# The order of projection, feed-forward openings and second mixer in a kernel of three transformer blocks

## What is computed

```python
def conv_ffn(h, w_up, conv_w, conv_b, w_down):
    u = h @ w_up                                   # 1024 -> 2 * 2816
    u = lax.conv_general_dilated(u, conv_w ...) + conv_b   # 3 taps, per channel, causal
    gate, val = jnp.split(u, 2, axis=-1)
    return (jax.nn.silu(gate) * val) @ w_down      # 2816 -> 1024

for i in range(2):                                 # i = 0: "fox", i = 1: "mla"
    h = rmsnorm(x, norm_mix[i])
    p = h @ w_in
    o_mix = mixer(p[..., :-MEM_WIDTH])             # 12 heads
    o_mem = memory_cross(p[..., -MEM_WIDTH:], k_mem, v_mem, ...)   # 4 heads, 256 keys
    x = x + jnp.concatenate([o_mix, o_mem], axis=-1) @ w_out[i]
    x = x + conv_ffn(rmsnorm(x, norm_ffn[i]), ...)
# the third block
x = x + 0.5 * swiglu(rms_norm(x, g_ffn1), ...)
x = x + mix(rms_norm(x, g_mix)) @ w_out            # window attention, 31-tap convolution, memory attention
x = x + 0.5 * swiglu(rms_norm(x, g_ffn2), ...)
```

## Time and profile before

| | |
|---|---|
| median of 3 runs | 2228.88 us (2228.45 to 2229.82) |
| the profiled execution: its own time | 2224.88 us |
| its span in the profile | 2223.1 us |
| TensorE busy | 2117.9 us, 95% |
| VectorE busy | 1274.8 us, 57% |
| ScalarE busy | 952.9 us, 43% |
| GpSimd busy | 33.7 us, 2% |
| mean granted TensorE clock | 0.982 |
| DMA | 187.36 MB, 84 GB/s on average |

### The profile page before, as it was taken

How to read it: one execution, slowest core, us unless ns; L and a number is a source line. 1 busy time by engine, 2 the same in 40 slices (tenths; PEclk the granted TensorE clock), 3 DMA queues, 4 the chain that set the end, 5 groups by cost and what they waited for, 6 DMA issues and landing times.

```text
span 2223.1 us, 30649 instructions
## 1 busy us (share of the span) xinstructions
PE 2117.9 (95%) x11378; PEld 1759.9 (79%) x11378; DVE 1274.8 (57%) x2212; ACT 952.9 (43%) x1912; POOL 33.7 (2%) x71
## 2 busy tenths in 40 slices
PE   6999998999999798989999999999998889999999
PEld 6888786888889676768888888888888667888887
DVE  6645567746764775567367544434447865543442
ACT  6645544423445764444244343223344564332331
POOL 0000001000000010000000000000001000000000
PEclk9999999999999899989999999999999999999999
DMA  6212132332333010222333233333232112333332
GB/s 203 73 53 58 49 91 62 102 103 90 95 100 105 15 39 29 71 76 95 100 94 100 95 95 100 95 97 98 90 100 62 39 30 81 105 99 91 103 96 91
DMA packets 101670, 187.36 MB, mean 84 GB/s; under 512 B 11408, under 2 KB 12048, under 8 KB 101264
## 3 DMA queue, kind: packets, MB, share of 16 engines
q1 hardware_dynamic: 101520, 185.39, 27.5%
HBM read 183.25 MB, written 2.10 MB: 83 GB/s over the span
## 4 chain that ended last, share of the span: by engine, by line
PE 47%; DVE 3%; ACT 2%; issue 1%; POOL 0%; DVEq 0%; ACTq 0%; POOLq 0%
PE PSA L1541 15%; PE PSA L1542 14%; PE PSA L1543 14%; PE PSA L1559 1%; PE PSA L1560 1%; PE PSA L1561 1%; DVE RS L1694 1%; DVE WL L1705 0%; ACT PP L2043 0%; ACT WH L1974 0%; PE PSA L1648 0%; PE PSA L1663 0%; DVE CV L1694 0%; PE PSA L1630 0%; DVE XT L1846 0%
## 5 line engine op out<-in xcount | busy, mean ns | idle before, releaser
L1705 DVE TENSOR_TENSOR WL<-RAW,WH 128x512 fp32r<-128x512 f32 x681 | 459.2, 690 | 470.7 <-ACT WH L1974 447.1
L1974 ACT ACTIVATE WH<-RAW 128x512 fp32r<-128x512 f32 x681 | 414.7, 626 | 485.5 <-PE PSA L1543 407.1
L1541 PE MATMUL PSA<-HNh,WH 128*128 128x512 f32 x1440 | 566.3, 393 | 28.5 <-DVE CV L1694 21.2
L1542 PE MATMUL PSA<-HNl,WH 128*128 128x512 f32 x1440 | 562.9, 391 | 0.0
L1543 PE MATMUL PSA<-HNh,WL 128*128 128x512 f32 x1440 | 562.8, 391 | 0.0
L1541 PEld LDWEIGHTS PSA<-HNh,WH 128*128 128x128 f32 x1440 | 272.0, 189 | 89.6 <-DVE CV L1694 22.0
L1542 PEld LDWEIGHTS PSA<-HNl,WH 128*128 128x128 f32 x1440 | 272.0, 189 | 57.3 <-issue 1.2
L1543 PEld LDWEIGHTS PSA<-HNh,WL 128*128 128x128 f32 x1440 | 271.8, 189 | 56.9
L1541 PE MATMUL PSA<-Gh,WH 128*128 128x512 f32 x704 | 274.3, 390 | 0.9 <-DVE Gl L1869 0.9
L1542 PE MATMUL PSA<-Gl,WH 128*128 128x512 f32 x704 | 273.9, 389 | 0.0
L1543 PE MATMUL PSA<-Gh,WL 128*128 128x512 f32 x704 | 273.9, 389 | 0.0
(11 more groups left out here) (253 smaller groups left out, 2478.1 us busy)
## 6 DMA issues: line engine op xcount, KB each, us to landing
RAW<-in_w SPq DMA_DIRECT2D x681, 256.0 KB, 2.6
XT<-in_x SPq DMA_DIRECT2D x8, 256.0 KB, 5.3
MT<-in_mem SPq DMA_DIRECT2D x2, 1024.0 KB, 6.4
out_x<-XT SPq DMA_DIRECT2D x8, 256.0 KB, 2.1
PAR<-in_par SPq DMA_DIRECT2D x1, 207.0 KB, 7.2
CB<-in_cb SPq DMA_DIRECT2D x1, 100.0 KB, 7.1
PAR<-in_par SPq DMA_DIRECT2D x1, 84.5 KB, 2.0
CONST<-in_const SPq DMA_DIRECT2D x1, 65.0 KB, 5.3
```

Source lines behind the costliest of these rows:

```text
L1541: pe.matmul(out, wh, xh, start=(a["start"] and c == 0), stop=False)
L1542: pe.matmul(out, wh, xl, start=False, stop=False)
L1705: dve.tensor_tensor(l[:, :], r[:, :], h[:, :], ALU.subtract).then_inc(done.sem("split.dve"), 1)
L1974: act.activation(h[:, :], r[:, :], ACT.Copy).then_inc(done.sem("split.act"), 1)
```

## The change

- Projection: chunks are closed in the order 0, 4, 1, 5, 2, 6, 3, 7 rather than 0 to 7. A chunk's square is put 5 beats and its addition 6.2 beats behind the closing of the chunk, rather than all behind the last chunk. The additions are chained in the order in which they are written, and `total` waits for the last of them.
- ffn 0, 1 and 3: one pair of groups is opened before the first `scale` rather than two, and `total` comes behind two groups rather than four (ffn 2 had it so). In later pairs each group is followed by its own `scale` and convolution, rather than both groups first.
- Second mixer: the memory queries' group comes before the latent group, its helper banks are 4 to 7, and memory attention begins directly behind the latent group.
- The value half of a key/value widening is emptied by VectorE (`vevac`) rather than by ScalarE, behind the key half; 12 instructions.
- `pbcast` is issued behind the values and the turns of that moment (`sums`), and the step of the attention sink earlier.
- Third mixer: some turns come 2.5 to 5 beats later.

```diff
 def out_parts(first, late):
-    return ([(c, first, late) for c in range(OPEN)] + [(c, late, 8) for c in range(OPEN)]
-            + [(c, first, 8) for c in range(OPEN, 8)])
+    return [(c, first, late) for c in range(OPEN)] + [x for c in range(OPEN) for x in ((c, late, 8), (OPEN + c, first, 8))]
...
             def add(self, c):
-                step("feed", (self.name, c), norm=self, c=c, sq=("feed", self.name, c))
+                step("feed", (self.name, c), norm=self, c=c, sq=("feed", self.name, c), last=self.adds[-1:])
+                self.adds.append(c)
...
-                if i == 3:
-                    need([("precip.dve", jkey)])
-                    aux = aux_bank(("pbcast", jkey), [("pspread.act", ckey)])
-                    step("pbcast", jkey, S=PSTAT[pstats.of[jkey]], bank=aux)
...
                 step("pvals", key, job=job, i=i, jkey=jkey, t=t)
-                return 0.3 * job.tiles[i][1] / 128 + (0.8 if i == 3 else 0)
+                return 0.3 * job.tiles[i][1] / 128
+
+            def sums(self, n, i):
...
+                step("pbcast", jkey, S=PSTAT[pstats.of[jkey]], bank=aux)
...
                     cost += self.values(*turned) if turned else 0
                     cost += self.turn(*scored) if scored else 0
+                    cost += self.sums(*turned) if turned else 0
...
                 norm.part(c, norm.free, 1.3)
+                after(5, lambda: norm.square(c))
+                after(6.2, lambda: norm.add(c))
...
             until([("part.dve", (norm.name, KC - 1))], 0)
-            for c in range(KC):
-                after(0.5 + 1.3 * c, lambda c=c: norm.square(c))
-                after(1.7 + 1.3 * c, lambda c=c: norm.add(c))
...
-                    if (s, q) == (0, 0):
-                        opened = [both(n) for n in range(ahead)]
-                    groups = opened[q] if q < len(opened) else both(q)
-                    for x, (g, b) in enumerate(groups):
...
+                    first = (s, q) == (0, 0)
+                    opened = [up_group(x) for x in range(2)] if first else []
+                    for x in range(2):
+                        g, b = opened[x] if first else up_group(x)
                         last.scaled(g, b)
...
-        ring[:], aux_ring[:] = [0, 1], [0, 1, 2, 3, 6, 7]
+        ring[:], aux_ring[:] = [0, 1], [4, 5, 6, 7]
...
+                if late:
+                    after(0.5, lambda: step("vevac", (g, t), copy=late(dst, t, PS[bank][:, 0:width])))
...
-                psum.take(("up", g, t), [("evac.act", (g, t))], bank)
+                psum.take(("up", g, t), [("vevac.dve" if late else "evac.act", (g, t))], bank)
...
-                 for x in range(2)], h, QR[:, 3 + p, :], 2.0)
+                 for x in range(2)], h, QR[:, 3 + p, :], 4.5)
...
+                elif k == "vevac":
+                    dst, src, root = a["copy"]
+                    w.wait_ge(*done("evac.act", key))
+                    dve.tensor_scalar(dst, src, root, None, ALU.mult).then_inc(done.sem("vevac.dve"), 1)
```

More of the change, by code:

```diff
@@ L618, in part @@
                 step("part", (self.name, c), norm=self, c=c, got=self.got[c], free=free, h=h)
-                self.out.append((h, l, [("part.dve", (self.name, c))]))
+                self.out[c] = (h, l, [("part.dve", (self.name, c))])
                 def low():
@@ L646, in finish @@
             def finish(self, free):
-                if not self.out:
+                if None in self.out:
                     for c in range(KC):
@@ L743, in rest @@
                         step("pmax", key + (xs.start,), job=job, i=i, xs=xs, S=S, tile=key, before=tokens, src=t.scores(xs))
+                    if i == 3 and job.sink is not None:
+                        step("psink", jkey, job=job, S=S, last=key + (0 if t.joint else 1,))
                     after(0.8 if job.both else 0, exponents)
@@ L807, in recip @@
                 S = PSTAT[pstats.of[jkey]]
-                if job.sink is not None:
-                    step("psink", jkey, job=job, S=S, last=(self.id, n, 3, 0 if self.at[self.id, n, 3].joint else 1))
                 step("precip", jkey, job=job, S=S, last=(self.id, n, 3))
@@ L825, in run @@
                         if scored or turned:
-                            yield (self.values(*turned) if turned else 0) + (self.turn(*scored) if scored else 0)
+                            yield ((self.values(*turned) if turned else 0) + (self.turn(*scored) if scored else 0)
+                                   + (self.sums(*turned) if turned else 0))
                             scored, turned = None, scored
@@ L876, in projection, with ffn @@
             until([("part.dve", (norm.name, KC - 1))], 0)
-            for c in range(KC):
-                after(0.5 + 1.3 * c, lambda c=c: norm.square(c))
-                after(1.7 + 1.3 * c, lambda c=c: norm.add(c))
-        def ffn(f, gate, up, down, layer, off, last, conv, weight, norm, between=None, ahead=1):
+        def ffn(f, gate, up, down, layer, off, last, conv, weight, norm, between=None):
             ring[:], aux_ring[:] = [0, 1, 2, 3, 4], [5, 6]
@@ L884, in ffn @@
             for s in range(2):
-                parts, opened = [], []
-                def both(q):
-                    c, key = HALF * s + q, (f, s, q)
-                    freed = [[("conv.dve", (key, x))] for x in range(2)] if conv else [[("silu.act", key)], [("gated.mul", key)]]
-                    return [dense(n, layer, col, last.out, t)
-                            for (n, col), t in zip(((gate, 128 * c), (up, off + 128 * c)), freed)]
+                parts = []
                 for q in range(HALF):
@@ L957, in wide, with up @@
             return g
-        def up(name, p, parts, copies, take, each):
+        def up(name, p, parts, copies, take, each, late=None):
             g, n0, cols = dense_at[0], tiles_at[0], up_cols(name, p)
@@ L1248, in lat_use @@
             after(6, key_squares)
+        mq_got, (banks, outs) = [("qsplit.dve", (g_mq, c)) for c in range(2)], halved([4, 5])
+        wide(norm, "mla", (0, 128), outs, banks, scaled(outs),
+             lambda g, Y, h: unscaled(g, by_heads(Y, 4), lambda h: ("evac.act", (g, h)), mq_chunks(0, par("mq1"))(Y), h,
+                                      QR[:, 1, :]),
+             take=take_y([y[:, :, :].rearrange("p a b -> p (a b)")[:, 0:1024].rearrange("p (t c) -> p t c", t=4)
+                          for y in YQ], 1), halves=2, lag=1)
         wide(norm, "mla", LAT_COLS, [PS[t][:, 0:416] for t in range(4)], range(4),
@@ L1282, in turn_pair @@
         def turn_pair(gq, gk, yq, yk_, p, ends):
-            w, free = places[p % 2], [("dense", g_mq)] if p < 2 else [att.last(2 + p - 2, "pscore.pe")]
+            w, free = places[p % 2], [("dense", g_lat)] if p < 2 else [att.last(2 + p - 2, "pscore.pe")]
             def go(x):
@@ L1718, in vector @@
                     w.wait_ge(*done("square.act", key))
-                    if c == 0:
+                    if not a["last"]:
                         dve.tensor_copy(nm.acc, S[:, 0:nm.N]).then_inc(done.sem("feed.dve"), 1)
                     else:
-                        w.wait_ge(*done("feed.dve", (nm.name, c - 1)))
+                        w.wait_ge(*done(*nm.fed(a["last"][0])))
                         dve.tensor_tensor(nm.acc, nm.acc, S[:, 0:nm.N], ALU.add).then_inc(done.sem("feed.dve"), 1)
```

67 lines of the change are left out of this document (37 added, 30 removed).

## The result

The changed kernel takes 2230.89 us (median of 12 runs, 2226.89 to 2232.95), the kernel before 2225.76 (median of 12 runs, 2223.05 to 2229.82). The ratio is 1.0019, 95% interval 1.0010 to 1.0028: about 0.2% slower, where 2212.4 was predicted. The profiled execution took 2232.69 of its own time against 2224.88, 7.8 more.

The account below looks back on a forecast made before the run. TensorE, busy 95% of the span, was taken as the bound, leaving its waits and half-clock stretches. Terms 3.8 + 9.4 - 4.7 + 2.6 + 0 + 2.0 + 3.4 = 16.5 us gained gave 2212.4 on the median's scale, range 2203 to 2223.

Parts of the forecast that it names:

- Second mixer: Second mixer's new order: waits for VG go (1.9 us), shorter waits for exponentials shrink (0.7), together 2.6 us gained.
- the values on VectorE: Second mixer: moving 12 value copies from ScalarE to VectorE changes nothing, 0 us.
- Broadcast of the sums: Mixers: values and turns fill about 0.7 us of each of three waits, 2.0 us gained.
- The forecast's bound on the bad side: Second mixer: at worst 4.9 us lost, one more wait for exponentials.
- The bound of 5.0: Values on VectorE: at worst 12 x 0.42 = 5.0 us lost.
- Third mixer: Third mixer: two waits for YC, 5.5 us in all, each 1.7 less by later turns, 3.4 us gained.
- Projections: Openings of feed-forward parts: low parts come later, 6.8 us lost in ffn 0 and ffn 3, 3.9 in ffn 1.
- ffn 0, 1 and 3: Feed-forward parts, projection delays included: ffn 0 gains 3.8 us, ffn 1 gains 9.4, ffn 3 loses 4.7.
- the signs of being wrong: Last low part of the first projection at 317, WL waits in up groups, or a mixer's memory part waiting longer.
- the 1.6 charged for VectorE: ffn 0: rotary angles make VectorE's rounds 0.4 us longer than TensorE's; four such rounds charged, 1.6 us.
- Rivals: Later low parts 2221.4 (0.13); VectorE bounds ffn 0, 1: 2219.3 (0.20); half clock 2239 (0.05); convolution stall stays 2238 (0.02).
- The one that ended slower (half clock at the openings): Feed-forward openings: waits leave TensorE at half clock through groups 1 and 2, 2239 us; chance 0.05.

Follow-up runs that it names:

- m_order: Changed kernel with the second mixer's latent group first again and the helper banks of before; ratio to before 0.9995.
- b_order: Kernel keeping mainly the gaining parts, with memory queries first, helper banks 4 to 7 and memory attention behind the latent group put back; one run, 2201.09 us.
- m_hold: Changed kernel with memory attention started only behind the first query and key/value widening, memory queries still first; ratio to before 1.0013.
- m_both: Changed kernel with the latent group first, helper banks of before, and values emptied by ScalarE again; ratio to before 0.9948.
- m_act: Changed kernel with the value half of the key/value widening emptied by ScalarE again; ratio to before 0.9995.
- v_lag0: m_order with the value copies on VectorE half a beat earlier, directly behind the key half; one run, 2222.64 us.
- m_sums: Changed kernel with the broadcast of the sums ahead of the values again and the sink's step in its old place; ratio to before 1.0026.
- p_only: m_both with the feed-forward function of before (two pairs opened, total behind four groups), projection as changed; one run, 2239.95 us.
- p_old: m_both with the output projections of before (closing order, squares and additions behind all parts), one pair still opened; one run, 2208.78 us.

## Why the prediction was wrong

It failed in the second mixer, by two terms, the order of its groups ("Second mixer") and the values on VectorE (put at 0), and to a smaller part in "Broadcast of the sums".

- **Second mixer, 2.6 gained.** The stage lost 15.9. I looked at the waits that stand in the list of before, and asked which of them would go. Those for `VG` did, but a wait of 2.34 for `KRT` at the second memory score took their place. The wait of 4.9 for exponentials, which the forecast kept, went too (they fell from 14.9 to 4.7 in all, the longest now 1.3), and that gain bought nothing. I did not ask what stands behind the moved work. In the order rows of the change the scores stand directly behind the latent group, and the widening groups "behind the first memory tiles". The widening begins a long chain (widening, head norms, turns, first score), and its end was moved 28 us back. Before, the memory queries' group covered the latent's chain ahead of it and memory attention the heads' chain behind it; after, memory attention is all there is for both. By m_order and b_order that costs 7.5 and 8.8 us up to the first score. m_hold, which moves memory attention alone, gives 1.6 back and shows 7.0 us of the latent's chain uncovered: it is the place of the latent group, with its helper banks, that costs. The forecast's bound on the bad side, one more wait of 4.9, was too narrow for the same reason. It priced one wait, and neither a chain nor the clock: 8.5 of the 15.9 are longer busy time of the same matmuls.
- **Values on VectorE, 0.** In the stage it lost 4.1 (m_order against m_both) to 6.9 (m_act against after), in the stretch up to the output projection 2.2 and 4.4. The bound of 5.0 that I kept was worked out from the copies' own time. Their place in VectorE's queue makes about half of the 2.2 (v_lag0): I named the queue in the projection, and not here. The two rows that I compared were also not like for like: 417 is a plain copy, 479 a scaled one. Plain copies take 417 on VectorE and 384 on ScalarE, scaled ones 477 and 479, so 417 against 479 doesn't say that VectorE is the faster one.
- **Broadcast, 2.0 gained over three mixers.** The first mixer lost some 4.4, the third gained about 5.5, the second moved by 1. The waits of before were in rows for all of them together, and I gave one answer for all.
- **Third mixer, 3.4 gained.** The stage gained 3.2, but by m_sums the broadcast made it, not the later turns: with the turns late and the broadcast early the stage took 206.3, more than before. The waits for `YC`, 5.5, are gone in after and in m_sums alike, and in both the scores wait 3.6 for `BQL` where they waited 1.0. The number was right by luck. No run puts the turns back alone.
- **Projections.** Right in ffn 0: late by 6.2 against 6.8, low part at 322.0 against 322.2, waits of 1.25 and 4.17 against 1.6 and 4.4. p_only has the loss alone, p_old its absence. In ffn 1 the last low part came 3.7 later in its stage, against 3.9, but TensorE was 5.1 behind at the end of the second group, 1.2 more than I charged.
- **ffn 0, 1 and 3.** -3.7, -9.1, +4.3 against -3.8, -9.4, +4.7. The stall for the fourth convolution went with the order of before, and comes back with it (p_only); whether by the two opened pairs alone, or also by the place of the scalings, was not parted. The sixth group of ffn 0 started at 346.3 on the clock of before, against 346.8. Of the signs of being wrong, one wait for `WL` in an up group did show, 0.9 in ffn 0, and fits the 1.6 charged for VectorE there.
- **Rivals.** None was it. The one that ended slower (half clock at the openings) had its place in the wrong stage: the half clock did grow, by 8 matmuls in ffn 0 (1.6 us, where the sum had 1.0), but most of it around the new waits of the second mixer.

The three feed-forward terms were right to 0.4 us, and the sign of the whole was wrong by a stage that I had given 2.6.

## What to carry to other kernels

When an order is changed, don't only list the waits that go: find the chains of the stage, and see where the change puts the first link of each and what is left to cover it. Price an instruction that is moved to an idle engine by what stands ahead of it in that engine's queue and by who waits for what it holds, not by its own duration alone. Compare stage by stage: here gains of 9, 4 and 3 us and losses of 16, 4 and 4 added up to a difference of 0.2%, and keeping the parts that gained without those that lost gave 1.1%.

## What was not expected of the hardware

A copy of the values from PSUM, 128x256 with a scale per partition, takes 477 ns on VectorE where the plain copy of that size takes 417, and 479 on ScalarE where the plain one takes 384. The scaled copies of the values also read 64 of every 128 columns; whether the scale or that makes the difference isn't shown. And of two waits of like length one was followed by slow matmuls and the other not: in ffn 1 of after a wait of 2.46 is followed by a matmul of 0.50 us, in before one of 2.37 by 0.80. In p_old the same wait of 2.37 is followed by 0.50, and a later one of 1.18 by 0.80:

```profile
916.29 0.50 PE L1554 MATMUL PSA<-HNh,WH 128*128 128x512 f32 x1 [2.37 <-DVE HNl L1707]
...
918.43 0.80 PE L1554 MATMUL PSA<-HNh,WH 128*128 128x512 f32 x1 [1.18 <-DVE HNl L1707]
```
